# A mixture-of-experts encoder layer: which batch of experts closes a turn of the loop

## The chip, the cores and the metric

The kernel runs on one core of a Trainium2 chip. The metric is the time of one execution on the device, in microseconds (us), as the median of several runs. Beside it there is a profile of one execution, in which each instruction of each engine and each packet of DMA has its time.

## The reference, cut to what matters

One layer of an encoder works on 256 tokens of 1024 numbers: an input projection, two parallel mixers (mLSTM and Mamba-2), an output projection, a LayerNorm, and then a mixture of experts. The change is in the last part alone. Each token is routed to 8 of 64 small experts; one shared expert takes all tokens:

```python
h = silu(xb @ w_gate[e]) * (xb @ w_up[e])        # w_gate, w_up: 1024 x 256
out = (h @ w_down[e]) * gate[:, None]            # w_down: 256 x 1024
y = y.at[tok].add(out)
```

The result is `layer_norm(ALPHA * h + routed + shared)`. All is float32, so an expert's weights are 3 MiB and all the routed experts' weights 192 MiB.

## The kernel before

**Batches.** The experts are taken in batches that fill the 128 columns of a TensorE tile: a batch of two experts gives each 64 places for tokens (a "wide" one), a batch of four gives each 32 (a "narrow" one). Which expert stands in which column of the table is worked out on the chip from the routing; experts with many tokens go to wide batches. `FIRST_B` = 20 batches (two of them of the shared expert) are written out one after the other; they end with narrow, wide, wide, narrow. Then a hardware loop takes turns of `TURN_B` = 6 batches each; how many turns there are depends on the routing, and here it is one. The list `TURN` (lines 445 to 447) gives the order of a turn's batches: a column of the table and a width each. `column` and `width` read it. `closes(b, turn)` is true for the last batch of a turn, `flushes` for that and the last batch ahead of the loop.

**Weights.** An expert's 3 MiB are cut into thirds of 1 MiB: part 0 holds the first half of gate and up together (k = 0 to 3), part 1 their second half (k = 4 to 7), part 2 the down weights. A third fills one of `PLACES` = 22 places in SBUF. `take` deals the thirds out to the places in a ring, in the order of the batches; `loads_of` says which thirds go in one DMA. In an ordinary batch of the turn that is parts 0 and 1 of each expert, then part 2 of each. SP issues all of them in order in one queue (`load_batch`), and waits ahead of each for the place's `free` semaphore, which TensorE increments when it is done with the third that lay there 22 thirds earlier.

The closing batch is loaded in smaller pieces, so that TensorE can follow the last bytes closely: part 0 in whole thirds, part 1 in halves (`last_up`, `full`), part 2 as one half (`last_down`) and two quarters (`last_piece`, `full`). The semaphores of those pieces are counted with `LAST`, the number of experts in the closing batch (lines 1245, 1322, 1351).

**TensorE.** `batch(b, turn, v)` first gathers the tokens of the next batch with one-hot matrices (L1144), then does gate and up of its own batch (L1258, 8 steps of k, each with one 512-column matmul per expert, the experts side by side in the array's columns), in whose middle it makes the transposed one-hot (L1269) and the gates (L1277). Then come the scatter of the batch before it (L1162), the transposes of the hidden layer (L1302) and the down matmuls (L1332). ScalarE applies SiLU (L1576) and copies the down results to `y_hi` (L1594, L1602); VectorE multiplies by the gate (L2019), sums the gate's parts (L2005, one reduction per expert) and makes the remainder `y_lo` (L1993).

In the closing batch the second half of down goes in two pieces of 256 columns, and between them the scatter of the first half. After the loop the second half's scatter, the LayerNorm on VectorE and the stores follow; the LayerNorm's weights are loaded behind the last piece, into a place that has come free.

Of the kernel before, what the change touches and what calls it, by code (L numbers as in the profile page):

```python
# [118 lines left out]

ROUTE_PE = 6  # L120
FRONT_PE = 8
LAST = 4
NPK = 24


def build(nc, a, out):
    ctx = ExitStack()
    with ctx:
# [306 lines left out]
        C0 = 4 * NARROW0  # L435
        W0 = NARROW + 2 * WIDE0
# [7 lines left out]
        BATCHES[SHARED_B:SHARED_B] = [(None, 1)] * T  # L444
        TURN = []
        for r in range(2):
            TURN += [(W0 + 4 * r + 2 * i, 2) for i in range(2)] + [(C0 + 4 * r, 4)]
        assert len(BATCHES) == FIRST_B and len(TURN) == TURN_B

        def static_at(b, turn):  # L450
# [21 lines left out]
        def closes(b, turn):  # L472

            return turn is not None and b == TURN_B - 1
# [71 lines left out]
        def home(b, turn, part, q):  # L546
            return spot[turn is None, b, part, q][0]
# [17 lines left out]
        ytmp = place[RESULT].rearrange("p (t n) -> p t n", t=T)  # L565
        assert all(home(TURN_B - 1, 0, part, q) not in (LN2_AT, RESULT) for part in range(PARTS) for q in range(LAST))

# [234 lines left out]
        def _(pe):  # L802
# [399 lines left out]
            def batch(b, turn, v):  # L1202
# [39 lines left out]
                for k in range(KD):  # L1242
                    part, c = k // 4, k % 4 * 512
                    if k == 4 and closes(b, turn):
                        pe.wait_ge(last_up, (turn + 1) * (16 * LAST))
                    elif c == 0 or (k == 6 and closes(b, turn)):
# [74 lines left out]
                if closes(b, turn):  # L1321
                    pe.wait_ge(last_down, (turn + 1) * (16 * LAST))
                else:
# [3 lines left out]
                def down(ps, c, n, last=False):  # L1327

                    for f in range(2):
                        for q in range(w):  # L1330
                            to, by = down_columns(ps, at_q[2][q], f, c, n)
                            mm = nc.tensor.matmul(to[rows[q]], phhT[:, f, rows[q]], by, start=(f == 0), stop=(f == 1))  # L1332
                            if last and f == 1:
                                mm.then_inc(free[at_q[2][q]], 1)
                    return mm
# [13 lines left out]
                if closes(b, turn):  # L1349

                    pe.wait_ge(last_piece, (turn + 1) * (16 * LAST))
                    down(bank[0], 512, 256).then_inc(down_piece, 1)
# [832 lines left out]
```

## Time and profile before

| | |
|---|---|
| time, median of 3 runs | 736.64 us (736.38 to 737.04) |
| profiled execution | 737.36 us, its span 735.5 us |
| granted clock of TensorE | 0.985 |
| PE (TensorE matmul) busy | 700.3 us, 95% of the span |
| PEld (weight load) busy | 406.1 us, 55% |
| DVE (VectorE), ACT (ScalarE) busy | 258.2 us, 166.3 us |
| DMA | 250.99 MB, mean 341 GB/s |

The span is the time from the first to the last instruction of that execution. PE's busy time counts a matmul from its start to its modelled end; matmuls overlap. In a row of the timeline the first number is the start in us from the start of the span, the second the length of the merged group; then come engine, source line, operation, what is written and read, the number of instructions, and in brackets the idle time before the group with what ended it. SPq is the queue in which SP issues its transfers.

### The profile page before, as it was taken

The page shows a single profiled execution, that of the slowest core. Times are in us where ns is not written, and L with a number is a line of the kernel's source. Part 1 is how long each engine was busy: PE and PEld are TensorE (multiplying, and loading weights), DVE is VectorE, ACT ScalarE, POOL GpSimd, SP SyncE. Part 2 cuts the span into 40 slices and gives each one's busy share as a digit, 9 for nine tenths or more (in the row PEclk, how much of TensorE's full clock was granted, in tenths as well). Part 3 has the DMA queues.
Part 4 walks back from the last instruction along what each step waited for, and adds up shares of the span by engine and source line. Part 5 has one row for each costly group of instructions (what it writes and reads, how often), then busy time and mean ns, then how long its engine had stood idle before and what let it go on. Part 6 is the DMA issues. An engine that isn't in the chain of part 4 may idle for free.

```text
span 735.5 us, 10923 instructions
## 1 busy us (share of the span) xinstructions
PE 700.3 (95%) x4398; PEld 406.1 (55%) x4398; DVE 258.2 (35%) x631; ACT 166.3 (23%) x344; POOL 47.5 (6%) x65
## 2 busy tenths in 40 slices
PE   9999999999999999999999999999989959998993
PEld 6888888888854455445444445444434424443441
DVE  0757675474638184222112211022212102221225
ACT  0210435157540053211111111111111111111111
POOL 1130023202020021000000000000000000000000
PEclk9999999999999999999999999999999989999997
DMA  8963544625389559999999999999999999999993
GB/s 341 405 225 134 180 165 171 229 97 184 120 361 402 222 210 365 381 390 421 424 426 425 423 436 426 418 435 426 426 431 432 423 426 421 426 425 425 414 405 150
DMA packets 30657, 250.99 MB, mean 341 GB/s; under 512 B 3968, under 2 KB 4256, under 8 KB 9872
## 3 DMA queue, kind: packets, MB, share of 16 engines
q1 hardware_dynamic: 27504, 240.78, 79.9%
q0 software_dynamic: 2448, 8.48, 3.4%
q10 hardware_dynamic: 656, 1.05, 0.5%
q8 instruction: 35, 0.57, 0.3%
q14 instruction: 14, 0.11, 0.0%
HBM read 249.31 MB, written 1.11 MB: 340 GB/s over the span
## 4 chain that ended last, share of the span: by engine, by line
PE 75%; DMA 11%; SPq 7%; DVE 4%; ACT 1%; issue 1%; DVEq 0%
PE bank L1258 20%; PE bank L833 20%; DMA arena<-in_we_dram 11%; PE bank L1332 7%; PE bank L976 7%; PE bank L1144 6%; PE bank L1162 4%; SPq L643 3%; PE bank L923 1%; SPq L631 1%; SPq L652 1%; PE bank L845 1%; SPq L645 1%; PE bank L1341 1%; PE bank L1302 1%
## 5 line engine op out<-in xcount | busy, mean ns | idle before, releaser
L1258 PE MATMUL bank<-arena 128*64 128x512 f32 (+2 forms) x1008 | 195.1, 613 | 14.8 <-DMA arena<-in_we_dram 14.8
L833 PE MATMUL bank<-arena 128*128 128x256 f32 x736 | 161.1, 380 | 0.0
L833 PEld LDWEIGHTS bank<-arena 128*128 128x128 f32 x736 | 139.4, 190 | 20.0 <-issue 1.2
L1258 PEld LDWEIGHTS bank<-arena 128*64 128x64 f32 (+2 forms) x1008 | 56.3, 128 | 111.8 <-issue 109.3
L1332 PE MATMUL bank<-arena 128*64 128x512 f32 (+2 forms) x496 | 84.4, 583 | 4.1 <-DMA arena<-in_we_dram 3.0
L1144 PEld LDWEIGHTS bank<-onehotb,h_part 128*128 128x128 bf16 x1152 | 64.5, 98 | 17.6 <-issue 17.6
L1144 PE MATMUL bank<-onehotb,h_part 128*128 128x128 bf16 x1152 | 68.4, 219 | 0.0
L1993 DVE TENSOR_TENSOR y_lo<-bank,y_hi 128x512 fp32r<-128x512 f32 (+1 forms) x49 | 33.3, 680 | 100.0 <-ACT y_hi L1594 75.7
L2005 DVE TENSOR_REDUCE arena<-bank 64x1 f32<-64x3 f32 (+1 forms) x64 | 10.1, 158 | 162.6 <-PE bank L1277 162.1
L976 PE MATMUL bank<-arena 128*128 128x512 f32 x128 | 55.3, 592 | 0.0
L1576 ACT ACTIVATE arena<-bank 128x256 f32<-128x256 f32 x26 | 10.0, 384 | 194.7 <-PE bank L1258 194.7
L1332 PEld LDWEIGHTS bank<-arena 128*32 128x32 f32 (+1 forms) x496 | 24.3, 122 | 52.6 <-issue 44.9
L1548 ACT ACTIVATE arena<-bank 128x512 f32<-128x512 f32 x54 | 32.2, 597 | 54.4 <-PE bank L1144 52.5
L976 PEld LDWEIGHTS bank<-arena 128*128 128x128 f32 x128 | 24.2, 190 | 29.7 <-issue 29.7
L1395 ACT ACTIVATE arena<-bank 128x512 f32<-128x512 f32 x24 | 14.3, 595 | 103.4 <-PE bank L833 103.4
L2019 DVE SCALAR_TENSOR_TENSOR arena<-arena,bank 128x256 f32<-128x256 f32 x26 | 12.4, 475 | 69.4 <-ACT arena L1576 69.4
L1689 DVE SCALAR_TENSOR_TENSOR arena<-arena 128x256 f32<-128x256 f32 x64 | 35.7, 557 | 2.3
L1162 PE MATMUL bank<-y_hi,onehotT 128*128 128x512 f32 x94 | 35.0, 445 | 0.0
L1594 ACT ACTIVATE y_hi<-bank 128x512 fp32r<-128x512 f32 x24 | 14.3, 598 | 89.8 <-PE bank L1332 88.5
L1162 PE MATMUL bank<-y_lo,onehotT 128*128 128x512 f32 x94 | 30.3, 394 | 0.0
L1431 ACT ACTIVATE bank<-arena 128x128 f32<-128x128 f32 x88 | 26.4, 353 | 1.6 <-DVE arena L1725 1.3
L736 POOL TENSOR_TENSOR arena<-arena,negm 128x512 f32<-128x512 f32 x20 | 23.6, 1204 | 33.5 <-DMA arena<-decay_rows 33.5
(290 smaller groups left out, 517.5 us busy)
## 6 DMA issues: line engine op xcount, KB each, us to landing
arena<-in_we_dram SPq DMA_DIRECT2D x79, 1024.0 KB, 16.1
arena<-in_we_dram SPq DMA_DIRECT2D x17, 3072.0 KB, 26.3
arena<-in_we_dram SPq DMA_DIRECT2D x23, 2048.0 KB, 27.4
arena<-in_wc_dram SPq DMA_DIRECT2D x15, 1024.0 KB, 11.5
arena<-in_wn_dram SPq DMA_DIRECT2D x8, 1024.0 KB, 4.7
arena<-in_wo_dram SPq DMA_DIRECT2D x8, 1024.0 KB, 4.7
apart<-in_we_dram SPq DMA_DIRECT2D x8, 1024.0 KB, 28.4
arena<-in_we_dram SPq DMA_DIRECT2D x12, 512.0 KB, 18.9
```

What stands on the lines that cost most here:

```text
L643: sp.dma_start(dst, src).then_inc(last_up if part == 1 else last_down, 16)
L736: nc.gpsimd.tensor_tensor(c if d == t else masked[i][:, d, :, :], c, negm[:, d:d + 1, :].to_broadcast([P, 4, P]), ALU.add).then_inc(rows_m ...
L833: mm = nc.tensor.matmul(bank[n % 2][:, j * S:(j + 1) * S], wk, xk, start=(k == 0), stop=(k == KD - 1))
L976: mm = nc.tensor.matmul(bank[2 * t + half][:, :], y[:, k, t * P:(t + 1) * P], w[:, c:c + 512], start=(k == 0), stop=(k == 2 * KD - 1))
L1144: mm = nc.tensor.matmul(bank[1 + half][:, (k % 4) * P:(k % 4 + 1) * P], h_part[i][:, t, k * P:(k + 1) * P], onehotb[v][:, t, :], start=(t ...
L1162: mm = nc.tensor.matmul(bank[4 + 2 * t + half][:, :], onehotT[v][:, t, :], part[:, half * 512:(half + 1) * 512], start=(first and part is ...
L1258: mm = nc.tensor.matmul(bank[0][rows[q], :], hc[v][:, k, rows[q]], place[at_q[part][q]][:, c:c + 512], start=(k == 0), stop=(k == KD - 1))
L1332: mm = nc.tensor.matmul(to[rows[q]], phhT[:, f, rows[q]], by, start=(f == 0), stop=(f == 1))
L1431: ex = nc.scalar.activation(to[:, j, :], row, ACT.Exp, bias=colT[:, (0 if diag else 4) + 2 * s + d, hd:hd + 1])
L1548: nc.scalar.activation(hc[v][:, 4 * half:4 * half + 4, :], bank[1 + half][:, :].rearrange("p (k c) -> p k c", k=4), ACT.Copy).then_inc(gat ...
L1689: ins = V.scalar_tensor_tensor(out=xbc[:, c, :], in0=xpad[:, c, k:k + S], scalar=convw[:, c, k:k + 1], in1=xbc[:, c, :], op0=ALU.mult, op1 ...
L1993: return V.tensor_tensor(y_lo[:, c], ps, y_hi[:, c].bitcast(F32), ALU.subtract)
```

## The change

In a turn of the loop the order of the batches becomes four, two, two, four, two, two in place of two, two, four, two, two, four. The same columns of the table are used, so the same experts are in batches of the same width. The closing batch, and with it `LAST`, has two experts in place of four.

```diff
@@ -119,7 +119,7 @@
 ROUTE_PE = 6
 FRONT_PE = 8
-LAST = 4
+LAST = 2
 NPK = 24
@@ -444,7 +444,7 @@
         BATCHES[SHARED_B:SHARED_B] = [(None, 1)] * T
         TURN = []
         for r in range(2):
-            TURN += [(W0 + 4 * r + 2 * i, 2) for i in range(2)] + [(C0 + 4 * r, 4)]
+            TURN += [(C0 + 4 * r, 4)] + [(W0 + 4 * r + 2 * i, 2) for i in range(2)]
         assert len(BATCHES) == FIRST_B and len(TURN) == TURN_B
```

## Rows read from the trace of the kernel before

**Rows 1.** The page's 40 equal slices: busy tenths, and what the DMA moved.

```profile
PE   9999999999999999999999999999989959998993
DMA  8963544625389559999999999999999999999993
GB/s 341 405 225 134 180 165 171 229 97 184 120 361 402 222 210 365 381 390 421 424 426 425 423 436 426 418 435 426 426 431 432 423 426 421 426 425 425 414 405 150
```

**Rows 2.** Waits: who waited for whom, us in total, times, longest us.

```profile
PE bank L1258 <- DMA arena<-in_we_dram: 14.8, 5, 8.0
```

**Rows 3.** Windows of the turn: busy by engine, PEclk, DMA share, GB/s.

```profile
601.00:672.00 71.00, 67.13 (x538) 30.45 (x540) 14.05 (x36) 11.09 (x20) 0.00 (x0) 0.98 1.01 424
672.00:702.00 30.00, 30.00 (x170) 12.97 (x168) 5.38 (x15) 3.76 (x7) 0.00 (x0) 0.94 1.01 418
```

**Rows 4.** Timeline of PE: the first gate/up group of batches, and one down.

```profile
542.83 6.20 PE L1258 MATMUL bank<-arena 128*32 128x512 f32 x40 [3.33 <-DMA arena<-in_we_dram]
...
560.80 4.51 PE L1258 MATMUL bank<-arena 128*64 128x512 f32 x20
...
601.38 1.07 PE L1258 MATMUL bank<-arena 128*32 128x512 f32 x2 [8.03 <-DMA arena<-in_we_dram]
...
620.28 4.51 PE L1258 MATMUL bank<-arena 128*64 128x512 f32 x20
...
636.39 4.51 PE L1258 MATMUL bank<-arena 128*64 128x512 f32 x20
...
652.57 0.62 PE L1258 MATMUL bank<-arena 128*32 128x512 f32 x2
...
671.66 6.21 PE L1258 MATMUL bank<-arena 128*64 128x512 f32 x20 [2.56 <-DMA arena<-in_we_dram]
...
689.54 4.51 PE L1258 MATMUL bank<-arena 128*64 128x512 f32 x20
...
699.34 3.65 PE L1332 MATMUL bank<-arena 128*64 128x512 f32 x16
...
705.71 0.62 PE L1258 MATMUL bank<-arena 128*32 128x512 f32 x2
```

**Rows 5.** Four transfers of the turn by source line: duration ns, issue us, time to landing.

```profile
L631 SPq DMA_DIRECT2D arena<-in_we_dram x1: 422/422/422, 591.7 to 591.7; - x1
...
DMA to landing us min/median/max: 30.6/30.6/30.6
...
L631 SPq DMA_DIRECT2D arena<-in_we_dram x1: 3407/3407/3407, 645.4 to 645.4; - x1
...
DMA to landing us min/median/max: 36.2/36.2/36.2
...
L631 SPq DMA_DIRECT2D arena<-in_we_dram x1: 1580/1580/1580, 669.7 to 669.7; - x1
...
DMA to landing us min/median/max: 31.7/31.7/31.7
...
L652 SPq DMA_DIRECT2D arena<-in_we_dram x1: 939/939/939, 712.1 to 712.1; - x1
...
DMA to landing us min/median/max: 9.8/9.8/9.8
```

**Rows 6.** Timeline of the closing batch, from its first down matmul.

```profile
716.85 1.92 PE L1332 MATMUL bank<-arena 128*32 128x512 f32 x16 [0.77 <-DMA arena<-in_we_dram]
...
719.46 0.69 DVE L1993 TENSOR_TENSOR y_lo<-bank,y_hi 128x512 fp32r<-128x512 f32 x1 [3.84 <-ACT y_hi L1594]
...
720.39 0.50 PE L1162 MATMUL bank<-y_hi,onehotT 128*128 128x512 f32 x1
...
722.04 1.07 PE L1332 MATMUL bank<-arena 128*32 128x256 f32 x16 [0.46 <-DMA arena<-in_we_dram]
```

**Rows 7.** Timeline of PE early in the expert stage: a down group.

```profile
326.53 3.64 PE L1332 MATMUL bank<-arena 128*32 128x512 f32 x32 [1.20 <-DMA arena<-in_we_dram]
```

**Rows 8.** The page's groups: busy us, mean ns of one, idle before.

```profile
L2005 DVE TENSOR_REDUCE arena<-bank 64x1 f32<-64x3 f32 (+1 forms) x64 | 10.1, 158 | 162.6 <-PE bank L1277 162.1
```

## The prediction

> **What bounds the kernel now.** I read the page's slices first. From the 19th of the 40 slices on, the DMA row stands at 9 and the rate at about 425 GB/s, until the last slice [rows 1]: the expert stage runs as fast as the weights arrive. TensorE also shows 9 tenths there, but the list of waits says that the gate/up matmuls (L1258) waited for weights five times, 14.8 us in all, up to 8.0 us at once [rows 2]. So TensorE has some slack, and the stream of weights has none: the windows give a DMA share of 1.01 at 424 GB/s from 601 to 672 us, and 1.01 at 418 GB/s from there to 702 us [rows 3].
>
> The timeline of TensorE shows why both are true [rows 4]. A batch of four and a batch of two cost TensorE the same, since four 32-column matmuls run beside each other where two of 64 columns do: from gate/up to the next gate/up, 652.57 - 636.39 = 16.18 and 705.71 - 689.54 = 16.17 us for a two, and 17.97 or 18.90 us for a four that began after a wait (560.80 - 542.83, 620.28 - 601.38; the latter also flushes two scatters). But a four has 12 thirds of 1 MiB to receive and a two has 6. From the issue and the landing of three transfers [rows 5]: 591.7 + 30.6 = 622.3, 645.4 + 36.2 = 681.6, 669.7 + 31.7 = 701.4 us. By the order of issue (the turn's thirds counted from 1) these end the 8th, 32nd and 40th third of the turn. That is (681.6 - 622.3) / 24 = 2.47 us a third: 29.6 us for a four, 14.8 us for a two. A two is bound by TensorE by 1.3 us, a four by the stream by more than 11 us. The order of the batches therefore decides which of the two ends last.
>
> In the kernel before, the last batch is a four. The two before it are twos, so TensorE catches up exactly there: it starts the closing gate/up at 705.71 without a wait, while thirds still land, and then follows the stream: the last piece lands at 712.1 + 9.8 = 721.9 us [rows 5] and the last down matmul starts at 722.04, after 0.46 us of waiting for it [rows 6]. The end is the stream's end plus a tail of scatters and LayerNorm.
>
> **The change part by part.** No expert, byte or matmul is added or taken away; the turn runs four, two, two, four, two, two.
>
> *What stays in place.* The stream has the same 48 thirds in the same 22 places, and SP issues them in one queue in order, so I take the n-th third to land when it landed before: the 8th at 622.3, 32nd at 681.6, 40th at 701.4. This holds only if SP is never short of a free place. Two fours now follow each other (the last before the turn and the first of it), 24 thirds in 22 places. When the first four of the turn can compute, at 622.4, its 4 down thirds and 10 thirds of later batches are ordered or on the way, 14 x 2.47 = 34.6 us of stream, and its gate/up frees 8 places well within its 18 us. So the cover is 34.6 us against at most 18, and I cost it at nothing; without that cover, each us that the 40th third is late is a us at the end. The bound from above is the longest wait for weights in the trace, 8.0 us [rows 2].
>
> *Where TensorE waits next.* The eight gate/up thirds of the first four are the turn's thirds 1 to 8: gate/up at 622.3 + 0.1 = 622.4, where a two began at 620.28 before. With 18 us for a four after a wait, it is done at 640.4. Two: its four gate/up thirds end at the 16th, 622.3 + 8 x 2.47 = 642.1; start there, done by 658.2 to 660.0. Next two: 22nd third at 656.9, no wait, done by 676.2 at the latest. Second four: the 32nd third, 681.6: a wait of over 5 us; with the 17.97 us of the four after a wait, done at 699.7. Third two: its gate/up ends at the 40th third, 701.4. So TensorE starts it at 701.5, after some 1.9 us of idle. Everything earlier is forgiven at this point: what counts is the 40th third.
>
> *The closing batch.* It can't begin before the third two is through: 701.5 + 16.17 = 717.65 us, against 705.71 before: +11.94. From gate/up to down a two without waits takes 699.34 - 689.54 = 9.80 us [rows 4]; the closing four took 716.85 - 705.71 = 11.14 with its waits for pieces [rows 4, 6]. So -1.34: down begins at 727.45, +10.60. By then all weights are there (before, the last landed at 721.9; eight closing thirds in small pieces took (721.9 - 701.4) / 8 = 2.56 us each, so half as many pieces may save 0.4 us that nobody waits for). The wait of 0.46 us ahead of the last down matmuls [rows 6] falls away. The one ahead of the second piece doesn't shorten the path: the scatter behind it waits for VectorE's y_lo, which ran from 719.46 to 720.15, and starts at 720.39 whatever the piece does. The down matmuls themselves cost the same for eight of 64 columns as for sixteen of 32 (equal batch times above). The rest, from the last down to the end, is the same work for two experts as for four.
>
> Sum: +11.94 - 1.34 - 0.46 = +10.1 us. The profiled execution took 737.36 us (span 735.5 and 1.86 around it), 0.72 us above the median of 736.64; +10.1 on the median is 746.8 us.
>
> *Cheap parts.* The closing batch has half the DMA issues in pieces, and two small reductions on VectorE in place of four: the issues are hidden behind transfers that are long queued, the reductions behind the second half of gate/up, so nothing. Uncovered, they would be worth the 0.4 us above and 2 x 158 ns [rows 8], both as gains. The LayerNorm weights are still loaded behind the last piece, one MiB or 2.5 us later, well ahead of their use.
>
> *The clock after the 1.9 us wait.* After waits of 2.56, 3.33 and 8.03 us TensorE's first 20 to 40 matmuls ran slow: 6.20 us where the same group takes 4.51 [rows 4], and the granted clock of 672 to 702 us is 0.94 [rows 3], part of it at 1.2 instead of 2.4 GHz. After a wait of 1.20 us the clock stayed, 3.64 us for 32 down matmuls [rows 7]. The wait ahead of the third two, 1.9 us, lies between. Its price is between 0 and 17.88 - 16.17 = 1.71 us, the two after the 2.56 us wait against the one after none. The middle of 1.20 and 2.56 is 1.88, so the rows don't settle it; I take 0, since the wait shrinks if the four before it is slower than 17.97 us, and keep 1.71 for the range. The slow clock of the earlier batches costs nothing, as the waits behind them take it up. The Trainium skill, page "TensorE: Matmul & The Clock Gate", section "HAM oscillation — how this bites in real kernels", tells of a matmul loop that waited for a transfer in every round and began every round at the low clock. By that rule the third two would begin slow as well, and the time would be that of the first rival. Three waits of this trace agree with it and the one of 1.20 us does not.
>
> **The rivals.** (1) The clock falls in the wait ahead of the third two: +10.1 + 1.7 = +11.8, 748.5 us. For it, the three waits above; against it, the shortness of this one. (2) The stream runs short at the two fours in a row. The price is between 0 and 8.0 us, passed on whole through the 40th third: 747 to 755 us. Against it, 34.6 us of queued transfers; for it, only that the trace never shows two fours side by side. (3) The other side: TensorE still keeps up with the stream, and a closing two ends with it. Then the gain is the smaller pieces, 0.4 us: 736.2 us, within what a measurement can tell. It needs the closing gate/up to begin by 705.7, so the third two's weights by 689.5, 12 us ahead of the 40th third in a queue that is already full; against it speaks every row of the stream. (4) A batch of two that is all in place runs quicker than 16.17 us: no row shows it; the three spans of twos without waits in [rows 4] are 16.11, 16.18 and 16.17 us.
>
> **How the numbers follow.** The forecast of 746.8 has 0.52, rival 1 0.28, rival 2 0.08, rival 3 0.06, rival 4 or another small gain 0.06. The range runs from 745.3 (a wait and a piece less than counted) to 749.8 (rival 1 and the low part of rival 2): it leaves out rivals 3 and most of 2 and 4, under 0.2 in all. The time can be told from no change from about 0.2%, 1.5 us, on. Rivals 1, 2, 4 and the forecast are all slower; rival 3 is the same, with a small part for faster.
>
> **What would show it.** Right: waits of gate/up for weights at about 622, 642, 682 and 701.5 us; then none; the closing gate/up at 717.6 and its down at 727.4, with the last third landed some 6 us before it; DMA idle from 722 on while TensorE is busy for 10 us more. Rival 1 shows in the third two's span, 17.9 instead of 16.2 us. Rival 2 shows as a DMA share under 1 between 600 and 700 us, or a 40th third after 702. Wrong altogether if the closing down still waits for its pieces, or if the third two starts well ahead of 701.

## The result, and the profile after

The changed kernel takes 743.67 us (743.42 to 744.34, four runs) against 736.51 us (736.10 to 737.04): 1.0100 of the time before, with a 95% interval of 1.0087 to 1.0113. So it is slower by 7.2 us, where 10.3 us over the same median were forecast (746.8), and it lies 1.6 us below the stated range. The profiled execution took 744.34 us, its span 742.5 us against 735.5: +7.0 us, and these are what the following accounts for.

The page's slices first, with what the DMA moved:

```profile
PE   9999999999999999999999999999989969897993
DMA  8963635544399478999999999999999999999981
GB/s 340 408 235 114 217 128 190 203 148 136 120 409 404 157 281 349 375 419 421 429 426 421 423 433 430 428 425 430 424 429 432 426 424 422 423 427 424 418 319 56
```

From the 19th to the 38th slice the stream runs as in [rows 1]. The last two slices have 319 and 56 GB/s where they had 405 and 150: the stream ends about when it did, and the kernel goes on without it. The windows around that end say it more closely (busy by engine, then PEclk, DMA share, GB/s), and below them the one behind the end of the stream in the kernel before:

```profile
702.00:721.00 19.00, 19.00 (x128) 8.60 (x126) 4.43 (x12) 2.77 (x5) 0.00 (x0) 1.00 0.95 378
721.00:731.00 10.00, 8.96 (x47) 4.23 (x44) 3.54 (x7) 2.10 (x5) 0.00 (x0) 1.00 0.04 15
```

```profile
722.00:731.00 9.00, 2.49 (x24) 1.56 (x24) 7.22 (x18) 1.96 (x4) 0.00 (x0) 0.80 0.06 25
```

From 721 to 731 us the DMA share is 0.04 and TensorE is busy for 8.96 of 10 us; before, from 722 to 731, it was busy for 2.49 of 9. The last piece of weights lands at 708.3 + 12.4 = 720.7 us. The timeline of TensorE has the batches' first gate/up group and the closing downs, to be held against [rows 4] and [rows 6]:

```profile
600.54 1.07 PE L1258 MATMUL bank<-arena 128*32 128x512 f32 x2 [8.32 <-DMA arena<-in_we_dram]
...
620.75 4.50 PE L1258 MATMUL bank<-arena 128*32 128x512 f32 x40
...
640.66 6.06 PE L1258 MATMUL bank<-arena 128*64 128x512 f32 x20 [3.29 <-DMA arena<-in_we_dram]
...
658.39 4.51 PE L1258 MATMUL bank<-arena 128*64 128x512 f32 x20
...
680.11 6.79 PE L1258 MATMUL bank<-arena 128*32 128x512 f32 x40 [5.44 <-DMA arena<-in_we_dram]
...
698.62 0.64 PE L1258 MATMUL bank<-arena 128*64 128x512 f32 x1
...
714.80 4.51 PE L1258 MATMUL bank<-arena 128*64 128x512 f32 x20
...
724.61 2.80 PE L1332 MATMUL bank<-arena 128*64 128x512 f32 x16
727.97 0.50 PE L1162 MATMUL bank<-y_hi,onehotT 128*128 128x512 f32 x1 [0.56 <-DVE y_lo L1993]
...
729.10 1.08 PE L1332 MATMUL bank<-arena 128*64 128x256 f32 x8
```

The last wait for weights stands at 680.11, ahead of the turn's second four; the turn's 32nd third is issued at 641.3 and lands 38.7 us later, at 680.0. From there on TensorE works off a four and two twos without another wait for a transfer: 18.51, 16.18 and 9.81 us to the closing down at 724.61. The third two starts at 698.62 with no idle time, not at 701.5 after 1.9 us of it. The transfers of its last two gate/up thirds, by source line (issue, then time to landing), tell why:

```profile
L631 SPq DMA_DIRECT2D apart<-in_we_dram x1: 2792/2792/2792, 665.2 to 665.2; - x1
...
DMA to landing us min/median/max: 32.8/32.8/32.8
...
L631 SPq DMA_DIRECT2D arena<-in_we_dram x1: 1957/1957/1957, 668.2 to 668.2; - x1
...
DMA to landing us min/median/max: 32.3/32.3/32.3
```

The pair of its second expert lies across the seam of the ring (place 21, which the trace calls `apart`, and place 0), so it went as two transfers. The first, the turn's 39th third, is part 0 and landed at 665.2 + 32.8 = 698.0; the second, the 40th, is part 1 and landed at 668.2 + 32.3 = 700.5 us. Line 1248 waits for part 0 at k = 0 and for part 1 only at k = 4, so the 39th third was enough to start.

### The profile page after: what moved, and what is told of

It reads as the page before. It is cut to its first block, busy times and chain, and to the rows that moved or that the text cites. A ratio compares the mean times of both kernels' runs of the same rounds, so it can differ in the third digit from the quotient of the medians.

```text
span 742.5 us, 10884 instructions
## 1 busy us (share of the span) xinstructions
PE 702.1 (95%) x4390; PEld 405.7 (55%) x4390; DVE 258.6 (35%) x631; ACT 166.4 (22%) x344; POOL 47.3 (6%) x65
## 4 chain that ended last, share of the span: by engine, by line
PE 76%; DMA 15%; DVE 4%; SPq 2%; ACT 1%; issue 1%; DVEq 0%
PE bank L1258 21%; PE bank L833 20%; DMA arena<-in_we_dram 15%; PE bank L1332 8%; PE bank L976 7%; PE bank L1144 6%; PE bank L1162 4%; SPq L631 1%; PE bank L923 1%; PE bank L845 1%; PE bank L1341 1%; PE bank L1302 1%; PE bank L947 1%; PE bank L1269 1%; DMA arena<-in_wc_dram 1%
## 5 line engine op out<-in xcount | busy, mean ns | idle before, releaser
L1258 PE MATMUL bank<-arena 128*64 128x512 f32 (+2 forms) x1016 | 198.0, 625 | 20.4 <-DMA arena<-in_we_dram 20.4
L1332 PE MATMUL bank<-arena 128*32 128x512 f32 (+2 forms) x480 | 84.1, 590 | 2.7 <-DMA arena<-in_we_dram 2.2
L2019 DVE SCALAR_TENSOR_TENSOR arena<-arena,bank 128x256 f32<-128x256 f32 x26 | 12.4, 476 | 69.0 <-ACT arena L1576 69.0
L1162 PE MATMUL bank<-y_lo,onehotT 128*128 128x512 f32 x94 | 30.3, 394 | 0.0
```

Source lines behind the costliest of these rows:

```text
L1162: mm = nc.tensor.matmul(bank[4 + 2 * t + half][:, :], onehotT[v][:, t, :], part[:, half * 512:(half + 1) * 512], start=(first and part is ...
L1258: mm = nc.tensor.matmul(bank[0][rows[q], :], hc[v][:, k, rows[q]], place[at_q[part][q]][:, c:c + 512], start=(k == 0), stop=(k == KD - 1))
```

## The experiments

Each edit is against the changed kernel unless it says otherwise; in them "theory A" is that the end hangs on the last four's weights and TensorE's work after them. Times are medians, with the ratio to the kernel before.

**Only the first half of the change (e1).** The turn runs four, two, two, two, two, four.

```diff
-LAST = 2
+LAST = 4
-            TURN += [(C0 + 4 * r, 4)] + [(W0 + 4 * r + 2 * i, 2) for i in range(2)]
+            pair = [(W0 + 4 * r + 2 * i, 2) for i in range(2)]
+            TURN += pair + [(C0 + 4 * r, 4)] if r else [(C0 + 4 * r, 4)] + pair
```

> The first half of the change alone: the turn runs four, two, two, two, two, four, so that two fours meet at the start of the turn, but a four closes it as before. Theory A (the loss lies at the end, where TensorE has three batches to work off after the last four's weights are there): the two fours side by side cost nothing, because TensorE waits and catches up over the twos; the closing four's gate/up begins within 2 us of the kernel before and its last down still follows the last landed piece, so 736.4 to 737.5 us. Theory B (the loss comes from the two fours side by side, which drain the places or the stream): 741 to 744 us, with a DMA share under 1 in the turn.

736.47 us, 1.0006 (0.9997 to 1.0015). Two fours in a row cost nothing. The closing four in the timeline of TensorE follows the pieces as in [rows 6]:

```profile
706.05 0.62 PE L1259 MATMUL bank<-arena 128*32 128x512 f32 x2
...
718.55 1.07 PE L1333 MATMUL bank<-arena 128*32 128x256 f32 x16 [0.68 <-DMA arena<-in_we_dram]
...
721.20 1.07 PE L1333 MATMUL bank<-arena 128*32 128x256 f32 x16 [0.43 <-DMA arena<-in_we_dram]
```

Theory B falls, and with it the prediction's rival of a stream that runs short there; in the changed kernel too the DMA share is 1.01 from 601 to 702 us.

**Only the second half (e2).** The turn runs two, two, four, four, two, two.

```diff
-            TURN += [(C0 + 4 * r, 4)] + [(W0 + 4 * r + 2 * i, 2) for i in range(2)]
+            pair = [(W0 + 4 * r + 2 * i, 2) for i in range(2)]
+            TURN += [(C0 + 4 * r, 4)] + pair if r else pair + [(C0 + 4 * r, 4)]
```

> The second half of the change alone: two, two, four, four, two, two, closing with a two. The last four batches, 24 thirds, are those of the changed kernel. Theory A: the second four still gets its gate/up weights with the 32nd third and TensorE still has that four and two twos to work off after it, so the same time as the changed kernel, 743.2 to 744.3 us. Theory B, that the meeting of fours at the start of the turn costs the time: that meeting is gone here and another one stands in the middle, so it would give either 736.5 us or, if any two fours in a row cost it, the same 743.7 us; together with the run of the first half this tells the two apart.

744.65 us (743.33 to 745.73), 1.0120 (1.0105 to 1.0134): the median is 0.35 us above what was expected, the interval overlaps that of the changed kernel. In its profile the second four begins at

```profile
679.63 6.23 PE L1259 MATMUL bank<-arena 128*32 128x512 f32 x40 [11.36 <-DMA arena<-in_we_dram]
```

after a wait of 11.36 us, twice that of the changed kernel and at the same place: what lies ahead of the second four adds nothing to the time that can be told from the scatter. With e1, the whole loss is in the second half of the change.

**The wait that the prediction had put there (e3).**

```diff
                     elif c == 0 or (k == 6 and closes(b, turn)):
+                        if turn is not None and b == 4 and k == 0:
+                            for q in range(w):
+                                pe.wait_ge(signal(b, turn, 1, q), landed(b, turn, 1, q))
                         for q in range(w):
```

> The changed kernel, with one wait more: the turn's third two begins gate/up only when all four of its gate/up thirds have landed, as the prediction had it, and not when the part-0 thirds have. Theory A (in the changed kernel it starts as soon as TensorE is done with the four, at 698.6 us, since it needs only the 39th third, landed at 698.0): the 40th third lands at 700.5, so its start moves by 2.0 us and the time with it, 745.4 to 746.0 us. Theory C (the stream's 40th third sets that start anyway): no change, 743.7 us.

745.58 us (745.46 to 746.43), 1.0127 (1.0112 to 1.0142), 1.5 to 1.9 us above the two measurements of the changed kernel, where 2.0 were expected. Beside e2 and e4, measured with it on one chip, it is 0.9 us higher, so the size is less sure than the direction. The start is where theory A has it:

```profile
700.69 0.64 PE L1261 MATMUL bank<-arena 128*64 128x512 f32 x1 [0.88 <-DMA arena<-in_we_dram]
```

The closing gate/up begins at 716.86, 2.06 us later than in the changed kernel's profile. With the wait that the prediction assumed, the time falls into its range.

**The third two's part 0 first (e4).**

```diff
+            if turn is not None and b in (4,):
+                return [[(part, q)] for part in (0, 1, 2) for q in range(w)]
             if turn is not None or b < WHOLE_FROM:
```

> The changed kernel, with the turn's third two loaded in single thirds, both part-0 thirds first: gate/up can begin with the 38th third, near 695.5 us, in place of the 39th, at 698.0. Theory A (TensorE's own work on the four sets that start): no change within 0.3 us, 743.4 to 744.0 us. Theory C (the landing of that batch's weights sets it): 2.5 us earlier, about 741.2 us.

744.63 us (743.74 to 745.22), 1.0114 (1.0099 to 1.0129); the median is 0.6 us above the band, and certainly not 2.5 us below. The profile has the second four and the third two where the changed kernel had them:

```profile
679.98 7.01 PE L1260 MATMUL bank<-arena 128*32 128x512 f32 x40 [7.01 <-DMA arena<-in_we_dram]
...
698.70 1.51 PE L1260 MATMUL bank<-arena 128*64 128x512 f32 x6
```

An earlier landing of the third two gives nothing: TensorE isn't free before. Theory C falls.

**The changed kernel again, beside the next three.**

> The changed kernel once more, as the common measure for the three that follow on the same chip: 743.4 to 744.6 us, about 1.0% above the kernel before.

744.07 us (743.50 to 744.34), 1.0106 (1.0091 to 1.0122).

**No idle time ahead of the second four (e5).**

```diff
                     pe.wait_ge(hidden_ready, p)
+                if turn is not None and b == 3:
+                    idle_front(24)
                 for k in range(KD):
```

> The changed kernel with 24 spare matmuls of 512 columns on TensorE ahead of the second four's gate/up, about 5.2 us of its 5.4 us wait for weights, so that the wait has no idle time and the clock stays at 2.4 GHz. Theory A: the four then takes 16.2 in place of 18.5 us and is done at 696.4, but the third two's 39th third lands only at 698.0, so that start moves by 0.5 us alone: 0.3 to 0.7 us less than the changed kernel. Theory D (only TensorE's own chain counts, and no landing stands close behind it): 2.3 us less.

744.29 us (743.63 to 746.27), 1.0107 (1.0091 to 1.0122): no gain, where 0.3 to 0.7 us were expected. The profile is of the slowest execution, 746.27 us, and shows where the gain went in that one:

```profile
673.03 5.34 PE L1032 MATMUL bank<-h_part,identb 128*128 128x512 bf16 x24
680.26 4.50 PE L1260 MATMUL bank<-arena 128*32 128x512 f32 x40 [1.89 <-DMA arena<-in_we_dram]
...
698.79 0.61 PE L1260 MATMUL bank<-arena 128*64 128x512 f32 x1 [2.10 <-DMA apart<-in_we_dram]
...
716.66 1.93 PE L1260 MATMUL bank<-arena 128*64 128x512 f32 x7
```

The four now runs at full clock, 4.50 us for the group that took 6.79 (granted clock 1.00 from 680 to 697 us; 0.87 from 680 to 699 in the changed kernel). But the wait has moved behind it: the third two waits 2.10 us for its 39th third (it lands in `apart`) and starts at 698.79, no earlier than in the changed kernel. Then it runs slow itself, 716.66 - 698.79 = 17.87 us. That is the prediction's first rival, at its price of 1.7 us; in the changed kernel the slow four leaves no wait there. The other three runs, 743.63 to 744.43 us, were not profiled.

**The same, and part 0 first (e6).** The edits of e4 and e5 together.

```diff
+            if turn is not None and b in (4,):
+                return [[(part, q)] for part in (0, 1, 2) for q in range(w)]
             if turn is not None or b < WHOLE_FROM:
...
                     pe.wait_ge(hidden_ready, p)
+                if turn is not None and b == 3:
+                    idle_front(24)
```

> The spare matmuls of the run before together with the third two's part-0 thirds loaded first. Theory A: now neither the clock nor the 39th third holds the third two; it starts at 696.4 with the four's end, 2.2 us ahead of the changed kernel, so about 2.2 us less. If the two edits just add (the loading order alone gave nothing to be told from noise): 0.5 us less.

742.58 us (741.65 to 743.23), 1.0085 (1.0071 to 1.0099): 1.5 us under the changed kernel on the same chip, where 2.2 were expected. In the profile the four takes 697.01 - 680.74 = 16.27 us and the two follows at once:

```profile
680.74 4.50 PE L1262 MATMUL bank<-arena 128*32 128x512 f32 x40 [1.81 <-DMA arena<-in_we_dram]
...
697.01 3.23 PE L1262 MATMUL bank<-arena 128*64 128x512 f32 x14
```

The changed kernel's four, beside it, took 17.91 us in its profile and not 18.51, so 1.6 was to be had. Two edits that give nothing each give 1.5 us together: two bounds stand less than 2 us apart, the four's end and the 39th third.

**Part 0 first in the second four too (e7).**

```diff
+            if turn is not None and b in (3, 4):
+                return [[(part, q)] for part in (0, 1, 2) for q in range(w)]
             if turn is not None or b < WHOLE_FROM:
```

> The changed kernel, with the second four and the third two both loaded in single thirds, part 0 of all experts first. Theory A: the four's gate/up can begin with the 28th third at 670.1, so TensorE goes on without its 5.4 us wait at 674.7, and stops only before the second half of gate/up until the 32nd third at 680.0; the four is done near 692, the third two starts with the 38th third at 695.5, and waits 0.4 us more for the 40th; 1.3 us less than the changed kernel if the clock falls in one of these waits, 2.6 us if not. If the end hung on TensorE's work after the last landed third alone, nothing would change.

742.49 us (741.86 to 744.12), 1.0092 (1.0078 to 1.0106), 1.6 us under the changed kernel's median, though the slowest run lies within that kernel's range. In its profile the four begins at 673.75 without the long wait, stops for 2.13 us ahead of its second half and for 1.72 us ahead of down, and the third two begins at 695.71:

```profile
673.75 3.64 PE L1260 MATMUL bank<-arena 128*32 128x512 f32 x32
...
679.52 1.06 PE L1260 MATMUL bank<-arena 128*32 128x512 f32 x8 [2.13 <-DMA arena<-in_we_dram]
...
680.85 4.32 PE L1260 MATMUL bank<-arena 128*32 128x512 f32 x24
...
695.71 3.65 PE L1260 MATMUL bank<-arena 128*64 128x512 f32 x16
```

The 24 matmuls at 680.85 take 4.32 us, where they take 2.78 at full clock: the clock fell (granted 0.76 from 679 to 686 us), the case for which 1.3 us were expected.

**The closing batch in whole thirds (e8).** Its loading follows the ordinary path, and TensorE waits for whole thirds.

```diff
-            if closes(b, turn) or (turn is None and b < PAIRED_FROM):
+            if turn is None and b < PAIRED_FROM:
...
-                    if closes(b, turn) and part > 0:
-                        break
...
-                if not closes(b, turn):
-                    return
+                return
...
-                    if k == 4 and closes(b, turn):
-                        pe.wait_ge(last_up, (turn + 1) * (16 * LAST))
-                    elif c == 0 or (k == 6 and closes(b, turn)):
+                    if c == 0:
...
```

> The changed kernel, with the closing two loaded like any other two, in pairs of thirds and whole down thirds, not in halves and quarters; its matmuls are as they were. Theory A: all its weights lie there 4 us before its down matmuls need them, so the pieces are worth nothing any more: the changed kernel's time, 743.5 to 744.5 us. If the end still hung on the last pieces: 1 us or more above that.

744.88 us (744.63 to 746.15), 1.0120 (1.0105 to 1.0136): 0.4 us above the band and 0.8 to 1.2 above the changed kernel's two medians, with intervals that overlap. Its profile gives no reason for that: the last third lands at 690.3 + 29.6 = 719.9, and the closing down starts at 724.90, 0.3 us from the changed kernel's. So no wait for weights is left that the pieces could shorten; whether whole thirds cost some tenths of a us stays open.

**Part 0 first in the kernel before (e9).** The same edit on the kernel before, in its first four and the two twos behind it.

```diff
+            if turn is not None and b in (2, 3, 4):
+                return [[(part, q)] for part in (0, 1, 2) for q in range(w)]
             if turn is not None or b < WHOLE_FROM:
```

> The kernel before (two, two, four, two, two, four), with the first four and the two twos behind it loaded in single thirds, part 0 of all experts first, the edit that took about 1.6 us off the changed kernel. Theory A: here the end is the last piece's landing and not TensorE's chain, so gate/up may start earlier in those batches and the time stays, 736.2 to 736.9 us. If TensorE's chain also set the end before: about 1.5 us less, 735 us.

736.96 us, 1.0007 (0.9998 to 1.0016). The closing gate/up begins 4.5 us earlier than in [rows 4], and gives it all back to the stream:

```profile
701.22 0.62 PE L1260 MATMUL bank<-arena 128*32 128x512 f32 x2
...
710.52 2.61 PE L1260 MATMUL bank<-arena 128*32 128x512 f32 x16 [2.88 <-DMA arena<-in_we_dram]
...
721.05 1.07 PE L1334 MATMUL bank<-arena 128*32 128x256 f32 x16 [0.25 <-DMA arena<-in_we_dram]
```

The same kind of edit takes 1.6 us off the changed kernel and nothing off the one before: the bound is another.

**One two behind the last four (e10).** The turn runs two, two, four, two, four, two.

```diff
-            TURN += [(C0 + 4 * r, 4)] + [(W0 + 4 * r + 2 * i, 2) for i in range(2)]
+            TURN += ([(W0, 2), (W0 + 2, 2), (C0, 4)], [(W0 + 4, 2), (C0 + 4, 4), (W0 + 6, 2)])[r]
```

> The turn two, two, four, two, four, two: it closes with a two as in the changed kernel, but one two, not two, stands behind the last four. Theory A (the end is the landing of the last four's gate/up weights plus TensorE's work on all that follows): those weights now end with the 38th third, near 695 us, in place of the 32nd, at 680; the four starts 15 us later, and one two of 16.2 us less follows it, so nearly the same time, 0.8 to 1.3 us less: 742.7 to 743.4 us. Theory E (each two at the end costs what it exceeds the stream's time by, 1.3 to 1.5 us, or half the loss): about 740 us.

743.21 us (743.06 to 743.55), 1.0092 (1.0077 to 1.0108), as theory A has it; theory E falls. The last four gets its weights 14 us later and has one batch less behind it:

```profile
694.52 7.31 PE L1258 MATMUL bank<-arena 128*32 128x512 f32 x40 [8.31 <-DMA arena<-in_we_dram]
```

## Why the prediction was wrong

**Right: what bounds each kernel.** Before, the stream's last piece set the end (e9, e1). After, it is TensorE's work behind the last four; the stream is over by 721 us, ahead of the closing down at 724.61. The direction and the mechanism hold, and what stands behind the last four decides (e1, e2, e10).

**Right: what costs nothing.** The two fours in a row (e1), everything ahead of the second four (e2, to within its scatter), and the pieces, of which no wait is left (e8, to about 1 us).

**Wrong: the first term of the sum.** "Third two: its gate/up ends at the 40th third, 701.4. So TensorE starts it at 701.5, after some 1.9 us of idle", and from it +11.94 us to the closing gate/up. It measured 714.80 - 705.71 = +9.09. The step took the third two's four gate/up thirds as one condition. They are two, part 0 at k = 0 and part 1 at k = 4, and the ring's seam splits exactly this pair, so its start asks for the 39th third (698.0), not the 40th. With that falls "Everything earlier is forgiven at this point": the four's own end, at 698.6, came after the 39th third and set the start. Of the 2.9 us, 2.0 is the wrong third. The other 0.9 is no effect of the change: in the profile of before the stream ran later than in any other here (a gate/up at 601.38 in [rows 4] that stands between 599.8 and 601.2 in the rest, at 600.54 in the changed kernel; the 40th third at 701.4 against 700.5). e3 puts the condition back: 745.58 us.

Put right with the prediction's own rows, the third two starts with the four's end at 699.7 (the 39th third is there at 698.9), 1.8 us earlier: a sum of +8.3 us and a forecast of 745.0. The rest is about those 0.9 us and the tail below. Two slips in the sums change nothing: the idle time of "some 1.9 us" is 701.5 - 699.7 = 1.8, and 701.5 + 16.17 is 717.67.

The same step had the first four wait at 622. It began at 620.75 without a wait, since its 7th and 8th thirds were two transfers as well (590.0 + 28.4 = 618.4 and 590.6 + 30.3 = 620.9). That cost the forecast nothing: the wait at 640.66 takes it up. Of the signs that the prediction named, the closing down without a wait and the idle DMA came, and so did its own sign of being wrong, a third two well ahead of 701.

**Nearly right: the closing batch.** Gate/up to down is 724.61 - 714.80 = 9.81 us, forecast 9.80. From there to the end of the span it is 742.5 - 724.61 = 17.89 us against 735.5 - 716.85 = 18.65, so -0.76 in place of -0.46. The first to the last down start makes 0.70 of it, 4.49 us against 5.19. The scatter between them starts 3.36 us after the first down (727.97), against 3.54 before: in [rows 6] it stood behind the late piece on TensorE as well, not behind VectorE's y_lo alone, as the prediction had it. In the kernel before the piece holds TensorE until 719.39 + 1.07 = 720.46, and the scatter starts at 720.39 (matmuls overlap), while y_lo was done at 720.15:

```profile
719.39 1.07 PE L1332 MATMUL bank<-arena 128*32 128x256 f32 x16 [0.61 <-DMA arena<-in_we_dram]
```

The three terms measured give +9.09 - 1.33 - 0.76 = +7.0 us.

**The clock.** The first rival didn't come true in the changed kernel's profile, but e5's shows it at its price, 17.87 us for 16.17. Where the prediction forgave a slow clock ahead of the third two, it counts: a second four at full clock takes 16.27 us (e6), 17.91 to 18.72 us in the profiles of the changed kernel, e2, e4 and e8, and 19.2 in e3.

The Trainium skill, page "TensorE: Matmul & The Clock Gate", section "HAM oscillation — how this bites in real kernels", tells of a loop that waits some 3 to 5 us for a transfer in every round and begins every round cold. The second four agrees with it (5.44 us of wait, 6.79 us for a group of 4.50). e5's third two began slow after a wait of 2.10 us, shorter than those, and the wait of 3.31 us below left the clock up; there the measurement decides. The prediction carried the page's loop over to a wait of 1.9 us, which is shorter than the page's waits.

No version here beats the kernel before. e6 and e7 lower the changed kernel's time by some 1.5 us and stay 0.9% above it.

## What to carry to other kernels

Where a stream of transfers and an engine bind in turns, put last the batch that the stream binds (here e1, 736.5 us, against e2, 744.7): work that is cheap to load and dear to compute, left to the end, is worked off when the stream is already over. To say when a batch can start, go through its waits one by one, which piece at which step, and look how the transfers were really cut; a ring's seam can hand out one piece early. Two bounds that stand 2 us apart must be moved together: each alone gave nothing here (e4, e5), both gave 1.5 us (e6).

## What the hardware showed that I had not expected

The length of a wait alone doesn't say whether the clock falls. In e3 a wait of 3.31 us left it up, and in e6 one of 1.94; in e5 one of 1.65 us was followed by slow matmuls (5.34 us for a group that takes 3.64), with a granted clock of 0.84 from 630 to 641 us:

```profile
640.71 4.51 PE L1261 MATMUL bank<-arena 128*64 128x512 f32 x20 [3.31 <-DMA arena<-in_we_dram]
```

```profile
641.31 4.51 PE L1262 MATMUL bank<-arena 128*64 128x512 f32 x20 [1.94 <-DMA arena<-in_we_dram]
```

```profile
631.07 5.34 PE L1334 MATMUL bank<-arena 128*32 128x512 f32 x32 [1.65 <-DMA arena<-in_we_dram]
```

e3's wait stands at a place where its program is still that of the changed kernel. The changed kernel's two profiles waited 3.29 us there and then took 6.06 and 7.42 us for the same group (granted clock from 640 to 652 us: 1.00 in e3, 0.86 and 0.74 in those two). So the price of one and the same wait differs between executions, here from 0 to 2.9 us. That e5's four runs lie as far apart as 743.63 and 746.27 us may come of that, but only one of them was profiled.
